# Stick-breaking attention: running sums on VectorE and transposed weights in place of matmuls with a triangle

## The reference, cut to what matters

```
for blk in range(S // SB_BLOCK):                 # 2 blocks of 128 queries
    qb, kb, vb = q[:, :, t0:t1], k[:, :, :t1], v[:, :, :t1]
    z = jnp.einsum('bhtd,bhsd->bhts', qb, kb) * scale
    mask = jnp.arange(t1)[None, :] < jnp.arange(t0, t1)[:, None]
    log_beta = jax.nn.log_sigmoid(z)
    log_keep = jnp.where(mask, jax.nn.log_sigmoid(-z), 0.0)
    rev = jnp.cumsum(log_keep[..., ::-1], axis=-1)[..., ::-1] - log_keep
    A = jnp.where(mask, jnp.exp(log_beta + rev), 0.0)
    outs.append(jnp.einsum('bhts,bhsd->bhtd', A, vb))
```

## Time and profile before

| | |
|---|---|
| median of 3 runs | 1692.2 us (1690.62 to 1693.33) |
| profiled execution | 1700.46 us, its span 1697.5 us |
| TensorE clock, mean over the span | 0.997 of full speed |
| PE busy | 1674.0 us, 99% |
| DVE busy | 1113.5 us, 66% |
| ACT busy | 783.5 us, 46% |
| POOL busy | 233.0 us, 14% |

### The profile page before, as it was taken

One profiled execution on the slowest core, in us unless ns is written; L12 is line 12 of the kernel. 1 busy time (PEld: TensorE's weight loads), 2 busy tenths in 40 slices (PEclk: granted clock), 3 DMA queues, 4 the chain that ended last, 5 costly groups with the idle time before them and its releaser, 6 DMA issues.

```text
span 1697.5 us, 27008 instructions
## 1 busy us (share of the span) xinstructions
PE 1674.0 (99%) x9836; PEld 1461.1 (86%) x9836; DVE 1113.5 (66%) x1157; ACT 783.5 (46%) x923; POOL 233.0 (14%) x153
## 2 busy tenths in 40 slices
PE   7999999999999999999999999999999999999998
PEld 6888888888888888888888888888888888888887
DVE  5765697777776665666656656666656666666664
ACT  6633444465553444434433345545554544444332
POOL 0000040000004510045100000000000005500164
PEclk9999999999999999999999999999999999999999
DMA  8566756555555554457566665555555555554463
GB/s 284 182 184 188 224 171 185 170 168 162 169 161 173 178 172 147 136 160 229 157 186 185 185 187 165 156 185 177 170 183 165 172 171 177 182 173 148 124 186 111
DMA packets 291924, 296.64 MB, mean 175 GB/s; under 512 B 8992, under 2 KB 288800, under 8 KB 291616
## 3 DMA queue, kind: packets, MB, share of 16 engines
q1 hardware_dynamic: 291872, 295.94, 56.1%
HBM read 293.81 MB, written 2.10 MB: 174 GB/s over the span
## 4 chain that ended last, share of the span: by engine, by line
PE 97%; DVE 1%; DMA 1%; ACT 0%; issue 0%; SPq 0%; DVEq 0%; ACTq 0%
PE ps L260 59%; PE ps L262 30%; PE ps L335 2%; PE ps L353 1%; DMA xv<-mem 1%; PE ps L282 0%; PE ps L502 0%; PE ps L492 0%; PE ps L483 0%; PE ps L395 0%; PE ps L418 0%; PE ps L450 0%; PE ps L445 0%; DVE wpair L794 0%; PE ps L344 0%
## 5 line engine op out<-in xcount | busy, mean ns | idle before, releaser
L794 DVE TENSOR_TENSOR wpair<-raw,wpair 128x1024 fp32r<-128x1024 f32 x544 | 698.7, 1297 | 355.7 <-ACT wpair L552 346.8
L552 ACT ACTIVATE wpair<-raw 128x1024 fp32r<-128x1024 f32 x544 | 571.6, 1059 | 718.0 <-PE ps L262 710.8
L260 PE MATMUL ps<-xpair,wpair 128*128 128x512 f32 x1920 | 680.2, 398 | 0.0
L260 PE MATMUL ps<-ypair,wpair 128*128 128x512 f32 x1536 | 542.5, 398 | 4.4 <-DVE ypair L881 3.0
L262 PE MATMUL ps<-xpair,wpair 128*128 128x256 f32 x1920 | 535.8, 279 | 0.0
L260 PEld LDWEIGHTS ps<-xpair,wpair 128*128 128x128 f32 x1920 | 360.4, 188 | 85.0 <-issue 0.6
L262 PE MATMUL ps<-ypair,wpair 128*128 128x256 f32 x1536 | 429.7, 280 | 0.0
L262 PEld LDWEIGHTS ps<-xpair,wpair 128*128 128x128 f32 x1920 | 361.8, 188 | 0.3
L260 PEld LDWEIGHTS ps<-ypair,wpair 128*128 128x128 f32 x1536 | 289.0, 188 | 75.1 <-issue 5.2
L262 PEld LDWEIGHTS ps<-ypair,wpair 128*128 128x128 f32 x1536 | 290.0, 189 | 0.1
L813 DVE TENSOR_REDUCE tmp<-ps 128x512 f32<-128x1024 f32 x136 | 166.3, 1223 | 66.8 <-PE ps L262 66.2
(11 more groups left out here) (180 smaller groups left out, 943.6 us busy)
## 6 DMA issues: line engine op xcount, KB each, us to landing
raw<-xa_wkv SPq DMA_DIRECT2D x128, 512.0 KB, 4.2
raw<-w_in_odd SPq DMA_DIRECT2D x128, 512.0 KB, 4.0
raw<-w_in_even SPq DMA_DIRECT2D x96, 512.0 KB, 3.6
raw<-xa_wq SPq DMA_DIRECT2D x64, 512.0 KB, 3.9
raw<-xa_wo SPq DMA_DIRECT2D x64, 512.0 KB, 4.3
raw<-w_out_even SPq DMA_DIRECT2D x32, 512.0 KB, 4.5
raw<-w_out_odd SPq DMA_DIRECT2D x32, 512.0 KB, 4.6
xv<-mem SPq DMA_DIRECT2D x8, 512.0 KB, 8.4
```

What stands on the lines that cost most here:

```text
L260: mm(bank, still[:, k, 0, tile], move[:, k].rearrange("p h n -> p (h n)"), start=(k == 0), stop=False)
L552: fn(wpair[:, KP * p:KP * (p + 1), 0, :], raw[:, p], ACT.Copy).then_inc(hi_ready, 1)
L794: v.tensor_tensor(wpair[:, kp, 1, :], raw[:, p], wpair[:, kp, 0, :].bitcast(F32), ALU.subtract).then_inc(lo_ready, 1)
```

## The change

Logits now have queries on the partitions and keys along the row: `sb_q` is the stationary operand and `sb_k` the moving one. A block of 128 queries by 128 keys and one of 128 by 256 stand side by side in the bank. The softplus is masked as before, with the mask turned round. The sum over keys is a reversed running sum on VectorE, along the row: one scan for each block of queries (L1135 of the new kernel), and then a subtraction from the logits in PSUM (L1140). The exponential is read from SBUF and masked as before. Since the value product needs keys on the partitions, TensorE transposes the weights, three 128 x 128 blocks a head (`turn`), and ScalarE copies them out of PSUM (`turned`). Two constant tables of 128 columns each go.

```
-                        mm(ps[:, 4 + h, 0:S], sb_k[:, h, 0:P], sb_q[:, h, :],
+                        mm(ps[:, 4 + h, 0:P], sb_q[:, h, 0:P], sb_k[:, h, 0:P],
                            start=True, stop=False, skip_group_check=True)
-                        mm(ps[:, 4 + h, S:S + P], sb_k[:, h, P:S], sb_q[:, h, P:S],
-                           start=False, stop=False, skip_group_check=True).then_inc(s["sb_z"], 1)
-
-                def cumulate():
-                    for h in range(2):
-                        pe.wait_ge(s["sb_sp1"], it * 2 + (h + 1))
-                        bank = ps[:, 4 + h, :]
-                        mm(bank[:, 0:S], const("neg_tri"), sb_sp[:, h, 0:S], ...)
-                        mm(bank[:, P:S], const("neg_ones"), sb_sp[:, h, S:S + P], ...)
-                        mm(bank[:, S:S + P], const("neg_tri"), sb_sp[:, h, S:S + P], ...
-                           skip_group_check=True).then_inc(s["sb_cum"], 1)
+                        mm(ps[:, 4 + h, P:3 * P], sb_q[:, h, P:S], sb_k[:, h, :],
+                           start=False, stop=True, skip_group_check=True).then_inc(s["sb_z"], 1)
+
+                def turn():
+                    for h in range(2):
+                        pe.wait_ge(s["sb_am"], it * 2 + (h + 1))
+                        for b in range(3):
+                            last = tr(ps[:, 4 + h, b * P:(b + 1) * P], sb_a[:, h, b * P:(b + 1) * P], ident)
+                        last.then_inc(s["sb_tr"], 1)
...
-                    pe.wait_ge(s["sb_am"], it * 2 + 2)
+                    pe.wait_ge(s["sb_at"], it * 2 + 2)
...
-                chunk(c + 3, 1, xpair, "T", hooks=((0, cumulate), (2, mix_values)))
+                chunk(c + 3, 1, xpair, "T", hooks=((1, turn), (3, mix_values)))
...
-                        act.wait_ge(s["sb_cum"], it * 2 + (h + 1))
-                        fn(sb_a[:, h, :], ps[:, 4 + h, 0:3 * P], ACT.Exp).then_inc(s["sb_aexp"], 1)
+                        act.wait_ge(s["sb_log"], it * 2 + (h + 1))
+                        fn(sb_a[:, h, :], sb_rc[:, h, :], ACT.Exp).then_inc(s["sb_aexp"], 1)
+
+                def turned():
+                    for h in range(2):
+                        act.wait_ge(s["sb_tr"], it * 2 + (h + 1))
+                        fn(sb_at[:, h, :], ps[:, 4 + h, 0:3 * P], ACT.Copy).then_inc(s["sb_at"], 1)
...
-                slot(c + 3, ((0, weights), (3, gate)))
+                slot(c + 3, ((0, weights), (1, turned), (3, gate)))
...
+                def cumulate():
+                    for h in range(2):
+                        dve.wait_ge(s["sb_sp1"], it * 2 + (h + 1))
+                        for first, last in ((0, P), (P, 3 * P)):
+                            rev = slice(last - 1, first - 1 if first else None, -1)
+                            ins = v.tensor_tensor_scan(sb_rc[:, h, rev], ones[:, 0:1].to_broadcast([P, last - first]),
+                                                       sb_sp[:, h, rev], 0.0, ALU.mult, ALU.add)
+                        ins.then_inc(s["sb_cum"], 1)
+                    for h in range(2):
+                        dve.wait_ge(s["sb_cum"], it * 2 + (h + 1))
+                        v.tensor_tensor(sb_rc[:, h, :], ps[:, 4 + h, 0:3 * P], sb_rc[:, h, :],
+                                        ALU.subtract).then_inc(s["sb_log"], 1)
...
-                slot(c + 2, ((1, softplus), (END, values)))
+                slot(c + 2, ((1, softplus), (2, cumulate), (END, values)))
```

More of the change, by code:

```diff
@@ L56 @@
 CONSTS = {}
-for _name, _n in (("ident", P), ("ones", P), ("neg_tri", P), ("neg_ones", P), ("sb_mask", 3 * P),
+for _name, _n in (("ident", P), ("ones", P), ("sb_mask", 3 * P),
                   ("hg_mask", P), ("reset", S)):
@@ L150, in build @@
         sb_l, sb_sp, sb_a = view(2048, 2, 3 * P), view(2816, 2, 3 * P), view(3584, 2, 3 * P)
+        sb_rc, sb_at = view(4352, 2, 3 * P), view(5120, 2, 3 * P)
         ident_in, const_in, x_in, pool_in, out_done = (sem(n) for n in ("ident_in", "const_in", "x_in", "pool_in", "out_done"))
@@ L167, in build @@
             xa_q xa_vhi xa_vlo xa_ptlo xa_scores xa_max xa_exp xa_rs xa_p xa_ptr xa_pt xa_pv xa_hi
-            sb_qr sb_kr sb_z sb_abs sb_exp sb_ln sb_sp0 sb_sp1 sb_cum sb_aexp sb_am sb_vr sb_av sb_gate sb_gsig sb_gg sb_y
+            sb_qr sb_kr sb_z sb_abs sb_exp sb_ln sb_sp0 sb_sp1 sb_cum sb_log sb_tr sb_at sb_aexp sb_am sb_vr sb_av sb_gate sb_gsig sb_gg sb_y
             fin_tr cs_zero""".split()
@@ L489, in cumulate @@
+                def turn():
                     for h in range(2):
-                        pe.wait_ge(s["sb_sp1"], it * 2 + (h + 1))
-                        bank = ps[:, 4 + h, :]
-                        mm(bank[:, 0:S], const("neg_tri"), sb_sp[:, h, 0:S], start=False, stop=False, skip_group_check=True)
-                        mm(bank[:, P:S], const("neg_ones"), sb_sp[:, h, S:S + P], start=False, stop=False, skip_group_check=True)
-                        mm(bank[:, S:S + P], const("neg_tri"), sb_sp[:, h, S:S + P], start=False, stop=True,
-                           skip_group_check=True).then_inc(s["sb_cum"], 1)
+                        pe.wait_ge(s["sb_am"], it * 2 + (h + 1))
+                        for b in range(3):
+                            last = tr(ps[:, 4 + h, b * P:(b + 1) * P], sb_a[:, h, b * P:(b + 1) * P], ident)
+                        last.then_inc(s["sb_tr"], 1)
@@ L497, in mix_values @@
                 def mix_values():
                     pe.wait_ge(s["sb_vr"], it + 1)
-                    pe.wait_ge(s["sb_am"], it * 2 + 2)
+                    pe.wait_ge(s["sb_at"], it * 2 + 2)
                     for h in range(2):
                         v = slice(h * P, (h + 1) * P)
-                        mm(ps[:, 6, h * S:(h + 1) * S], sb_v[:, 0, v], sb_a[:, h, 0:S],
+                        mm(ps[:, 6, h * S:(h + 1) * S], sb_v[:, 0, v], sb_at[:, h, 0:S],
                            start=(h == 0), stop=False, skip_group_check=True)
-                        last = mm(ps[:, 6, h * S + P:(h + 1) * S], sb_v[:, 1, v], sb_a[:, h, S:S + P],
+                        last = mm(ps[:, 6, h * S + P:(h + 1) * S], sb_v[:, 1, v], sb_at[:, h, S:S + P],
@@ L1263, in constants @@
         "ones": np.ones((P, P)),
-        "neg_tri": -1.0 * (p >= j),
-        "neg_ones": -np.ones((P, P)),
-        "sb_mask": np.concatenate([p < j, np.ones((P, P)), p < j], 1),
+        "sb_mask": np.concatenate([p > j, np.ones((P, P)), p > j], 1),
         "hg_mask": (p <= j) & (p // HC == j // HC),
```

## The result

The changed kernel takes 1714.8 us (median of 4 runs, 1713.08 to 1719.86) against 1691.8 before (4 runs). The ratio is 1.0129, 95% interval 1.0102 to 1.0155: slower, by 22 to 23 us (the ratio gives 21.8, the difference of the medians 22.9). The forecast was 1710.8, 1.1% slower. The profiled execution took 1713.64 us, its span 1711.8.

A forecast was written before the change was run, and what follows sets the result against it. The prediction took TensorE's stream, 97% of the chain, as the bound: profiled 1700.46 + 15.2 (longer iterations) + 3.4 (clock falls) = 1719.1 us, less 8.3 to the median gives 1710.8 us; range 1702 to 1721.

The forecast's parts named there:

- The wait: In the loop, after piece 1, TensorE waits 2.6 us an iteration for VectorE's mask of the weights.
- The prediction's sign: In the profile after, TensorE's transposes wait for VectorE's mask 16 times, twice an iteration, 20 to 24 us in all.
- VectorE's new instructions: Four scans and two subtractions in VectorE's queue between the split of piece 2 and the take: 2.76 us together.
- The rival of dear scans: A reversed scan on VectorE costs twice a forward one, the mask is 1.8 us later: 1725 us, chance 0.05.
- The iteration's growth: Piece 2 begins at 1234.24 instead of 1232.30, so each loop iteration is 1.9 us longer, 15.2 us in eight.
- The level: The profiled execution stands 8.3 us above the median of the runs, taken off the sum of 1719.1 us.
- The clock: TensorE's clock falls 2 times in the 8 iterations, in the stretch between pieces 1 and 2: 2 x 1.7 = 3.4 us.
- it falls every time: The clock falls in all eight iterations because transposes don't hold it up: 13.7 us, time 1721 us, chance 0.12.
- The rival on the other side: Head 1's mask ends before TensorE finishes piece 1, only the shorter stream is left: faster, 1684.6 us, chance 0.05.
- TensorE's saving: On TensorE the cumulation's 1.75 us goes and six transposes of 0.80 come: 0.95 us an iteration, 7.6 in eight.

The follow-up runs named there:

- many_transposes: late_turn with each group of three transposes done seven times over, 42 in a row without a wait: 1721.8 us.
- double_scans: The changed kernel with each of the four running sums done twice, the first time into an unused tile: 1743.0 us, ratio 1.0304 to the kernel before.
- late_turn: The changed kernel with the transposes and ScalarE's copies behind piece 2 of the gate chunk instead of piece 1: 1693.5 us, ratio 1.0006 to the kernel before.

## Why the prediction was right

- **The wait** took the place of the cumulation, at the place and by the queue that the prediction named. Forecast 2.6 us an iteration, measured 2.41 in the fifth and 2.6 at the longest, 19.7 over the loop. The prediction's sign was 16 waits of 20 to 24 us in all; the list has eight, just under that. The second head's transposes follow the first's without a wait of their own; from the first transpose to the next piece it is 0.77 us (1238.76 to 1239.53), where 0.82 was reckoned. VectorE's new instructions were 2.73 us (2.76). The reversed scan costs what a forward one does: 663 and 407 ns for 256 and 128 elements, against 679 forward at 256 and 400 estimated at 128:

```profile
L1135 DVE TENSOR_TENSOR_SCAN scratch<-cst,scratch 128x256 f32<-128x256 f32 x16 | 10.6, 663 | 0.0
L1135 DVE TENSOR_TENSOR_SCAN scratch<-cst,scratch 128x128 f32<-128x128 f32 x16 | 6.5, 407 | 0.0
```

  The rival of dear scans falls.
- **The iteration's growth** was forecast from pairs at 347 ns. With that pace ahead of the transposes the gap is 3.90 us, 1.88 more than the cumulation's 2.02; forecast 1.9. With slow pairs the wait is shorter by what the pairs take longer, so this part costs the same. The 8 x 1.9 = 15.2 us stand (8 x 1.88 = 15.0).
- **The size that was off** is what the sum didn't hold: the pace of pairs, a term that the prediction does not have. The iteration grew by 2.49 us, of which the gap explains 1.88; the other 0.61 are the pairs between the other breaks, each some 6.6 ns slower, or 4.9 us if all eight iterations have it. 15.0 + 4.9 = 19.9, and one fall of the clock 1.4 to 1.7: 21 to 22 us, against 22 to 23 measured and 18.6 forecast. The lower mean clock of the other three executions can hold the rest. That the slow pace belongs to the change is not shown: the traces of the loop speak for it, the differences in unchanged code and between two executions of one kernel for chance.
- **The level** of the forecast was the profiled execution less 8.3 us, its distance from the median. The slower pace and the fall of the clock ahead of the loop, 6 us in all, belong to that execution, so most of what was taken off was rightly taken off.
- **The clock**: two falls in eight at 1.7 us were forecast, one in each trace was seen, and the one that was reckoned cost 1.35 us. Both falls came at a gap with fast pairs ahead of it, where TensorE waited 2.61 us; of the five gaps like that in the two traces two had a fall, of the eleven with 2.4 us of wait none:

```profile
1032.41 1.54 PE L493 MATMUL ps<-cst,scratch 128*128 128x128 f32 x6 [2.61 <-DVE scratch L1146]
```

  The number of falls was an interpolation between two rows, and that it came out close is in part luck, since its reason was wrong: it counted the transposes as if they were idle time. So did the rival "it falls every time", which did not happen. The Trainium skill says that transposes don't count as a busy TensorE in the same way ("TensorE: Matmul & The Clock Gate", Part 4). As far as keeping the clock up goes, many_transposes, with 4.6 us of them at a clock of 1.00 throughout, does not agree, and the measurement decides; whether transposes alone would raise the clock no run shows. double_scans shows the fall every time when TensorE waits 4.2 us. What set off the fall of the earlier trace rows stays open: in the changed kernel's first trace the same transposes have a longer wait among them, and the clock stays at 1.00:

```profile
807.43 0.63 PE L283 MATMUL ps<-cst,xv 128*128 128x128 f32 x4 [2.06 <-DVE ypair L845]
```

- **The rival on the other side** (faster, 1684.6) needed the mask of head 1 some 3 us earlier (it was reckoned at 1233.84 against 1230.79) or TensorE later. late_turn does the latter and has no wait, yet comes out level: TensorE's gap did shrink by 0.90 us, 7.2 in all, but slower pairs took 3.7 us of it in the loop and 1.9 behind it. TensorE's saving is real, and in this kernel the pace of the pairs takes most of it.

## What to carry to other kernels

When one engine's stream is the time, work that moves from it to a queue with idle time is not free: add up what stands in that queue ahead of the instruction that the bound engine waits for, and compare the moment it ends with the moment at which the bound engine (here TensorE) arrives. If it is late by a microsecond or two, let the bound engine meet it one piece later (here this brought back 21 of the 22 to 23 us) or move the awaited instruction ahead in its queue (12 us). And keep such waits short: the wait of 4.2 us cost the clock as well, in eight of eight.

## What the runs showed of the hardware that was not expected

- The same pairs of matmuls (512 and 256 columns) run at 347 or at 353 ns, at the same granted clock. In all 13 traces the pace of the long stretches (80 pairs and more) is constant from one break in the stream (a hook, a wait) to the next, hundreds of pairs on end, and changes only there. It can differ between two executions of the same code: 568 pairs of the memory projections were at 353 and 353 ns in the two traces of the kernel before, and at 347 and 353 in the two of the changed one. All of them at one pace or the other is 3.8 us of this kernel. What picks it stays open.
- Transposes in a dense row start 0.11 us apart, and for the 4.6 us of 42 of them the granted clock stayed at 1.00 (2.4 GHz), in eight of eight iterations.
- A reversed running sum costs as much as a forward one (663 against 679 ns for 256 elements), about 2 ns an element.
